# Four stages of the next top-k ahead of the first dot at a switch to a new piece

## The reference

```
q = (xb @ w_q), 8 heads of two halves
s1, s2 = scores of the halves against 128 sub-keys each
t1, i1 = top_k(s1, 16); t2, i2 = top_k(s2, 16)
top, sel = top_k(t1[..., :, None] + t2[..., None, :], 16)    # of 256 candidates
idx = (i1 * 128 + i2)[sel];  g = softmax(top)
a = gelu(einsum('thkd,td->thk', expert_u[idx], xb))
y = einsum('thk,thkd->td', g * a, expert_v[idx])
```

## Time and profile before

| | |
|---|---|
| median of 3 runs | 3385.03 us |
| lowest, highest | 3380.8, 3386.82 us |
| the profiled execution | 3354.33 us |
| its span in the trace | 3352.6 us |
| busy: PE, DVE, POOL, ACT | 70%, 64%, 59%, 16% |
| mean granted TensorE clock | 0.74 |
| HBM read, written | 1180.69 MB, 14.15 MB |

### The profile page before, as it was taken

The page is one execution under the profiler, slowest core; times in us unless marked ns, Lnnn a source line. Parts: engine busy times, 40 slices in busy tenths (PEclk is TensorE's granted clock), DMA queues, the critical chain, the costliest instruction groups (busy, mean ns, idle before and its releaser), DMA issues.

```text
span 3352.6 us, 42363 instructions
## 1 busy us (share of the span) xinstructions
PE 2349.4 (70%) x15147; PEld 1174.5 (35%) x15147; DVE 2147.1 (64%) x5579; ACT 535.9 (16%) x1059; POOL 1992.9 (59%) x2128
## 2 busy tenths in 40 slices
PE   8995775667667888877857765668567765675545
PEld 4652352335233533334534432325223431221111
DVE  1257757776676656657577667676676676766653
ACT  2211111211121221112121111111111111210001
POOL 0036666666666566665666666666666666666665
PEclk9996796678566988987867776678676875566555
DMA  6479999999999999999999999999999999999998
GB/s 229 149 277 405 358 349 375 362 373 349 375 357 381 368 402 408 408 400 357 362 353 365 366 369 363 360 372 351 376 361 374 364 353 377 359 359 362 368 368 325
DMA packets 348955, 1197.59 MB, mean 357 GB/s; under 512 B 37760, under 2 KB 54408, under 8 KB 346952
## 3 DMA queue, kind: packets, MB, share of 16 engines
q0 software_dynamic: 304128, 1107.43, 87.8%
q1 hardware_dynamic: 44616, 87.45, 7.1%
HBM read 1180.69 MB, written 14.15 MB: 356 GB/s over the span
## 4 chain that ended last, share of the span: by engine, by line
PE 31%; issue 16%; POOL 14%; DVE 13%; DMA 10%; another core or an unknown queue 9%; DVEq 5%; ACT 1%; ACTq 0%; SPq 0%; POOLq 0%
PE mx L1574 9%; PE acc L1675 7%; POOL ring L597 7%; POOL ring L586 7%; DVE ring L1273 6%; DMA ring<-in_peer_v_dram,idx 4%; PE mx L1385 3%; DMA ring<-in_peer_u_dram,idx 3%; DVEq L1145 2%; PE acc L1361 2%; PE mx L1585 2%; PE mx L1556 1%; DMA weights<-in_w_in_dram 1%; PE h2p L1628 1%
## 5 line engine op out<-in xcount | busy, mean ns | idle before, releaser
L1273 DVE SCALAR_TENSOR_TENSOR ring<-ring,h2p 128x1024 f32<-128x1024 f32 x1056 | 1272.2, 1214 | 551.7 <-DMA ring<-in_peer_u_dram,idx 267.5
L1675 PE MATMUL acc<-ring,wk 128*32 128x256 f32 x8448 | 1030.7, 507 | 684.6 <-DMA ring<-in_peer_v_dram,idx 317.5
L597 POOL DMA_INDIRECT ring<-in_peer_v_dram,idx x1056 | 995.3, 942 | 790.6 <-remote 369.4
L586 POOL DMA_INDIRECT ring<-in_peer_u_dram,idx x1056 | 995.8, 943 | 554.7 <-issue 302.4
L1675 PEld LDWEIGHTS acc<-ring,wk 128*32 128x32 f32 x8448 | 316.5, 129 | 1316.5 <-issue 776.9
L1574 PE MATMUL mx<-reg,weights 128*128 128x128 f32 x1792 | 275.3, 309 | 42.4 <-issue 42.1
L1574 PEld LDWEIGHTS mx<-reg,weights 128*128 128x128 f32 x1792 | 245.8, 216 | 101.5 <-issue 101.1
L1556 PE MATMUL mx<-weights,reg 128*128 128x512 f32 (+1 forms) x256 | 138.6, 668 | 1.9 <-DVEq L1246 1.1
L1385 PE MATMUL mx<-weights 128*128 128x512 f32 (+1 forms) x288 | 132.4, 604 | 2.2 <-issue 1.4
L1628 PE MATMUL h2p<-ch,ident 32*32 32x512 f32 x528 | 104.4, 798 | 31.2 <-issue 20.2
L828 ACT ACTIVATE gl<-dots 128x16 f32<-128x16 f32 x66 | 14.2, 216 | 537.8 <-issue 368.5
(11 more groups left out here) (311 smaller groups left out, 2425.6 us busy)
## 6 DMA issues: line engine op xcount, KB each, us to landing
ring<-in_peer_u_dram,idx POOLq DMA_INDIRECT x1056
ring<-in_peer_v_dram,idx POOLq DMA_INDIRECT x1056
weights<-in_peer_w_q_dram SPq DMA_DIRECT2D x7, 2048.0 KB
weights<-in_w_in_dram SPq DMA_DIRECT2D x5, 2048.0 KB, 18.2
weights<-in_w_in_dram SPq DMA_DIRECT2D x10, 1024.0 KB
ring<-in_peer_w_q_dram SPq DMA_DIRECT2D x8, 1024.0 KB, 6.1
xt<-in_x_prompt_dram SPq DMA_DIRECT2D x8, 512.0 KB
ring<-in_w_out_dram SPq DMA_DIRECT2D x2, 2048.0 KB, 13.6
```

Source lines behind the costliest of these rows:

```text
L586: pool.indirect_dma_start(ring[:, U_AT[n % NU], :], None, u_d, bass.IndirectOffsetOnAxis(ap=idx[:, g % 4, k:k + 1], axis=0)).then_inc(u_in ...
L597: pool.indirect_dma_start(ring[:, V_AT[n % NV], :], None, v_d, bass.IndirectOffsetOnAxis(ap=idx[:, g % 4, k:k + 1], axis=0)).then_inc(v_in ...
L1273: V.scalar_tensor_tensor(ring[:, U_AT[n % NU], :], ring[:, U_AT[n % NU], :], 1.0, h2p[:, :], ALU.mult, ALU.mult, accum_out=dots[:, (g + 1) ...
L1675: last = T.matmul(sums[g // 2 % 2][j * SUB:(j + 1) * SUB, :], wk[:, n // FEW % 5, n % FEW, :], ring[:, V_AT[n % NV], j * QD:(j + 1) * QD], ...
```

## The change

A constant `AHEAD = 4` is added. At the switches named `ahead` (but not at g = 5, where no stage is done before the dot in either kernel) VectorE computes stages 0 to 3 of the next top-k between `weigh(g)` and the first dot, in place of stage 0. Behind the dots k = 1 to 7 of these groups it then computes stage k + 3, in place of stage k behind the dots 1 to 10. All other groups keep their order.

```diff
+AHEAD = 4
@@ VectorE, before the first dot
                     if ahead:
                         weigh(g)
                         if g != 8 - 3:
-                            topk(g + 3, 0)
+                            for stage in range(AHEAD):
+                                topk(g + 3, stage)
                     if k == 0 and g % 2:
                         dve.wait_ge(h2p_set, (g + 1) // 2 + 1)
                     dve.wait_ge(u_in[n % NU], 16 * (n // NU + 1))
@@ VectorE, behind a dot
                     elif g == 8 - 3:
                         if k >= 5:
                             topk(g + 3, k - 5)
-                    elif k <= 10 and g + 3 < GROUPS and g != 8 * FIRST - 3 and not ahead:
+                    elif g % 2 and g < GROUPS - 3 and g != 8 * FIRST - 3:
+                        if 0 < k and k + AHEAD - 1 <= 10:
+                            topk(g + 3, k + AHEAD - 1)
+                    elif k <= 10 and g + 3 < GROUPS and g != 8 * FIRST - 3:
                         topk(g + 3, k)
```

## The result

The change makes the kernel slower. After: 3397.28 us median (3392.73 to 3402.83, 7 runs); before, on the same chip, 3386.71 (3380.8 to 3392.51, 7 runs). The ratio is 1.0032, 95% interval 1.0022 to 1.0042. The forecast was 3366.4 us, faster; the measured time lies just inside the upper end of its range, 3398, which stood for the late first dots.

The account below looks back on a forecast made before the run. No engine was full; a shared chain bound it, VectorE at most 18%. Gain 21.7 us less 3.1 us lost at one switch gives 18.6 us: 3385.0 to 3366.4 us, range 3330 to 3398.

Parts of the forecast that it names:

- the late first dots: Rival: stages 1 to 3 outlast short h2p waits, GpSimd stands still behind the late dot; 13.3 us slower, 3398.3 us, chance 0.17.
- 8 × 3.03 = 24.2 us gained: Gain from taking three stages from behind the first dot at eight switches; 21.7 us after 2.5 us for one late dot.
- the eight stretches: Eight switches where the chain stays on VectorE from the first dot to some 25 us on, so stages are on the path.
- from dot 11 on all start 3.0 us sooner: Behind a changed switch, dots from 11 on were to start 3.0 us sooner, as stages 1 to 3 no longer follow the first dot.
- heavy stages three dots sooner: Stages 8 and 9 move behind dots 5 and 6; dots 7 and 8 start some 0.8 us later, unfelt if GpSimd paces.
- The other 22 waits are 3.18 us or more, and their first dot keeps its time: At 22 of 29 changed switches the wait for h2p was to hide the 3.1 us of stages moved ahead.
- So where the chain leaves VectorE within a few dots I take nothing: At switches where another engine soon holds the chain, an earlier dot was to bring no gain, as GpSimd's rows set the pace.
- off-the-path case: Rival: time won on VectorE ends in waits for u rows; time unchanged at 3385.0 us, chance 0.25.
- 13.3 us: Summed lateness of first dots at the seven switches whose h2p wait is under 3.1 us.
- or if the eight stretches gain nothing: Second condition for the slower rival to decide; the first was more than seven of 29 waits under 3.1 us.
- The full sum: Rival: VectorE ends each piece sooner, the spread starts sooner and all switches gain; 74.6 us faster, 3310.4 us, chance 0.13.
- Not what it says: Rival: "one dot sooner" is three dots by the code; priced within the forecast, no time or chance of its own.

Follow-up runs that it names:

- c2: The change at g = 3, 7, 13, 33, 37, 41, 45, 55 alone, all other switches as in the kernel before; ratio to before 1.0000.
- c1: The changed kernel run again, nothing altered; ratio to the kernel before 1.0012.
- b3: Changed kernel with stages 0 to 3 ahead of the first dot, but stages 4 to 10 behind dots 4 to 10; ratio to before 0.9995.
- e2: The change only at the 11 switches without a VectorE mixer step behind dots 0 to 10, others as before; ratio to before 1.0001.
- c3: Changed kernel with stages 1 to 3 behind the first dot in place of ahead of it; ratio to before 1.0020.
- d2: Kernel before with stage 0 still ahead of the first dot, but stages 1 to 10 packed behind dots 1 to 7; ratio to before 1.0012.
- c4: Kernel before with stage 1 and two FIND_INDEX8 of stage 2 dropped at the odd groups, nothing put ahead; ratio to before 0.9979.
- e3: The change only at the 18 switches with a VectorE mixer step behind one of dots 0 to 10, others as before; ratio to before 1.0018.
- d4: Changed kernel with stages 0 to 3 ahead of the first dot, but stages 4 to 10 behind dots 9 to 15; ratio to before 1.0017.
- b1_before: The kernel before run again unchanged, for a second profile; ratio to before 1.0000.
- f2: Kernel before with no stage ahead of the first dot at the 29 switches, stages 0 to 10 behind dots 5 to 15, second run; ratio 0.9990.
- e4: Kernel before with no stage ahead of the first dot at the 29 switches, stages 0 to 10 behind dots 5 to 15, first run; ratio 0.9987.
- d3: Kernel before with stage 0 ahead of the first dot, but stages 1 to 10 behind dots 6 to 15; ratio to before 0.9995.

## Why the prediction was wrong

**The step that failed** is "8 × 3.03 = 24.2 us gained" in the eight stretches. c2 has it alone and gains nothing (1.0000; the eight pieces 0.3 us longer in all), and the two first traces, from the slower chip, do not show the gain either: there these eight pieces are 6.6 us longer in all. Two things were wrong in it. The gain was counted from the first dot ("from dot 11 on all start 3.0 us sooner"), but the first dot itself is later (2.3 us in the mean in c1), and from the old piece's last dot the balance is a loss up to dot 9 and about zero from dot 12 on. And I took VectorE's share of the chain in the earlier trace rows as a sign that less work anywhere in the stretch shortens it. In the two pieces that could be followed (14 and 2), what stands on the path is one mixer step behind a certain dot, and what precedes that step counts. I named the two facts that decide (heavy stages three dots sooner; mixer hand-overs) and did not lay one over the other, which the lists of slots allow without a trace.

**"The other 22 waits are 3.18 us or more, and their first dot keeps its time"** failed: seven more grew by 3 us on the first chip, where VectorE's own stages and the spread both stalled longer, and nearly all on the others, where the waits are not there. Each wait in the earlier trace rows was taken as a property of the kernel; it was one of that execution. The price of a late dot was overrated in turn: with 70 us more of gaps the change loses 3 to 6 us, and b3 with 69 us more loses nothing.

**"So where the chain leaves VectorE within a few dots I take nothing"** held more widely than I used it (piece 23; e2).

**The rivals.** The off-the-path case holds for most pieces: u-row waits grew. The late first dot has the right sign for this kernel, and 13.3 us is near the 10.6 measured, which is luck; its condition "or if the eight stretches gain nothing" was met. But its mechanism, GpSimd standing still behind the late dot, is not what costs: b3 and e2 have the late dots without the loss, c3 and d2 the loss without late first dots. The full sum is excluded by c4, where 41 us brought 5.7. "Not what it says" had no time of its own; it should have had one, since b3, which differs from after in this alone, is 0.15% faster.

**Shown and not shown.** Shown: the loss of 0.10 to 0.18% on the later chips comes from the switches that have mixer steps and not from the late first dots (e2, e3, b3, c3); in piece 14 a hand-over 1.6 us late makes 2 of the 3 to 6 us, and in piece 2 the length follows another hand-over. Not shown: which steps make the rest, and why eight of these switches by themselves lose nothing (c2). Not shown either: why the loss was 0.32% in the first comparison. There the hand-over of piece 14 is 1.7 us later too (16.06 against 14.40), but the piece only 0.3 us longer; piece 2 is 6.6 us longer, with its `h2_copy` 4.7 us late. Four of VectorE's 17 stalls after lie where the change packs short instructions, but none of the five later groups had stalls, so they couldn't be tested; and one trace of each kernel there can't separate cause from chance.

## What to carry to other kernels

Count a move of work from the last event that is the same in both orders, not from the first one behind it, and list for each hand-over to another engine what stands ahead of it: a step is late until the moved work has been given back. Where transfers pace a stretch, the time of single steps in it is nearly free, and only hand-overs out of it are worth a place. So the work that nobody waits for belongs behind them, but not ahead of the next one: in d4 it made `h2_copy` late. Before a wait is filled, see in a second execution, on another chip if there is one, that it is there.

## What was not expected of the hardware

- The same kernel took 3386.71 us in the first comparison and 3112 to 3113 us in five later ones, on four chips; why is not known. Piece 23 moved 364 GB/s (2391 to 2471 us, before) against 406 here; TensorE's v steps (line 1675) stood idle for 305.5 us that nothing visible ended in the first trace of before, and in b1_before they waited mainly for rows:

```profile
L1675 PE MATMUL acc<-ring,wk 128*32 128x256 f32 x8448 | 881.5, 514 | 861.4 <-DMA ring<-in_peer_v_dram,idx 758.7
```

- The chain that ended last is another one there. b1_before:

```profile
DMA 38%; PE 26%; POOL 14%; DVE 12%; issue 7%; DVEq 4%; ACT 1%; SPq 0%; ACTq 0%; POOLq 0%
```

  against DMA 10% and issue 16% in the earlier trace rows. The Trainium skill (Perfetto Trace Analysis, Optimization Strategy) says that a kernel can have regimes with different most-contended engines. The traces agree: gathers in piece 23 (DMA share 1.03), VectorE and TensorE in the hand-over of piece 14.
- A hand-over that came 3.8 us sooner (piece 14 of f2) shortened the piece by 6.4 us. TensorE's granted clock was 1.00 in it in place of 0.52, so that its matmuls ended 8.8 us sooner (16.3 us behind the last dot in place of 25.1); e4 has the same. In d3, 11.3 us behind the last dot, these matmuls had a mean clock of 0.64, and in all traces with the hand-over at 14.3 us or later 0.50.
